# A hybrid attention and pooling layer on one core: key and query splits in other slots of GpSimd, VectorE and ScalarE, and a token load later in the first up step

## The reference, cut to what matters

```python
h = rmsnorm(x, norm1_g)
proj = h @ w_in                      # 8 query heads, 2 key and 2 value heads of 64, and 512 pooling columns
q = apply_axial_rope(rmsnorm(q, q_norm_g), cos, sin)
k = apply_axial_rope(rmsnorm(k, k_norm_g), cos, sin)
a = block_swept_gqa(q, k, v)         # softmax(q k^T / 8) v, bidirectional, 4 query heads share a key head
p = multiscale_pool(u, w_pool, pool_scale)
x = x + jnp.concatenate([a, p], axis=-1) @ w_out
h2 = rmsnorm(x, norm2_g)
x = x + jnp.square(jax.nn.relu(h2 @ w_up)) @ w_down
```

## Time and profile before

| what | before |
|---|---|
| median of 3 runs | 1506.07 us |
| lowest and highest | 1505.72 and 1506.11 us |
| the profiled execution's own time | 1507.0 us |
| its span, first to last instruction | 1505.2 us |
| TensorE busy | 1492.5 us, 99% of the span |
| VectorE, ScalarE, GpSimd busy | 68%, 48%, 26% |
| granted TensorE clock, mean | 1.000 |

### The profile page before, as it was taken

One profiled execution on the slowest core, in us unless ns is written; L12 is line 12 of the kernel. 1 busy time (PEld: TensorE's weight loads), 2 busy tenths in 40 slices (PEclk: granted clock), 3 DMA queues, 4 the chain that ended last, 5 costly groups with the idle time before them and its releaser, 6 DMA issues.

```text
span 1505.2 us, 23418 instructions
## 1 busy us (share of the span) xinstructions
PE 1492.5 (99%) x8035; PEld 1329.2 (88%) x8035; DVE 1018.7 (68%) x1287; ACT 717.6 (48%) x1212; POOL 391.7 (26%) x344
## 2 busy tenths in 40 slices
PE   9999999999999999999999999999999999999999
PEld 8999977888878889999999999999888888888887
DVE  7434489999975668445445444547888878888875
ACT  6323278999943445545455455546333223223220
POOL 3356368888950000000000000000411311311300
PEclk9999999999999999999999999999999999999999
DMA  6110021000054747533432433338743443443434
GB/s 241 46 34 18 18 84 36 12 14 10 15 189 168 256 154 290 233 127 115 151 138 111 152 120 122 130 137 309 277 154 107 145 153 98 142 158 93 149 99 181
DMA packets 68969, 195.19 MB, mean 130 GB/s; under 512 B 5544, under 2 KB 7728, under 8 KB 68784
## 3 DMA queue, kind: packets, MB, share of 16 engines
q1 hardware_dynamic: 66848, 183.36, 34.8%
q10 hardware_dynamic: 2064, 11.08, 1.8%
HBM read 119.97 MB, written 67.63 MB: 125 GB/s over the span
## 4 chain that ended last, share of the span: by engine, by line
PE 58%; DVE 0%; issue 0%; ACT 0%; DVEq 0%; ACTq 0%
PE ps L786 19%; PE ps L788 19%; PE ps L787 19%; DVE wulo L1706 0%; DVE hout L2091 0%; DVE wuraw L2033 0%; DVE yacc L2172 0%; ACT hout L1533 0%; ACT u L1221 0%; DVE u L2079 0%; DVEq L2076 0%; DVEq L2087 0%; DVEq L2236 0%; ACTq L1516 0%; DVEq L2077 0%
## 5 line engine op out<-in xcount | busy, mean ns | idle before, releaser
L786 PE MATMUL ps<-h,wuhi 128*128 128x384 f32 (+1 forms) x904 | 301.5, 334 | 1.0 <-ACT u L1221 0.8
L788 PE MATMUL ps<-h,wulo 128*128 128x384 f32 (+1 forms) x904 | 301.1, 333 | 0.0
L787 PE MATMUL ps<-h,wuhi 128*128 128x384 f32 (+1 forms) x904 | 301.1, 333 | 0.0
L786 PE MATMUL ps<-wdhi,hidhi 128*128 128x512 f32 x672 | 261.5, 389 | 0.0
L788 PE MATMUL ps<-wdhi,hidlo 128*128 128x512 f32 x672 | 261.5, 389 | 0.0
L787 PE MATMUL ps<-wdlo,hidhi 128*128 128x512 f32 x672 | 261.4, 389 | 0.0
L2165 DVE TENSOR_TENSOR yacc<-yacc,ps 128x1024 f32<-128x1024 f32 x167 | 203.3, 1217 | 77.6 <-PE ps L788 77.5
L1221 ACT ACTIVATE hidhi<-hin 128x1024 fp32r<-128x1024 f32 (+1 forms) x72 | 86.8, 1206 | 301.0 <-PE ps L788 292.0
L2079 DVE TENSOR_TENSOR u<-u,ps 128x384 f32<-128x384 f32 x96 | 53.1, 553 | 183.0 <-PE ps L788 178.5
L786 PEld LDWEIGHTS ps<-h,wuhi 128*128 128x128 f32 x904 | 169.7, 188 | 2.0 <-issue 1.4
L787 PEld LDWEIGHTS ps<-h,wuhi 128*128 128x128 f32 x904 | 169.7, 188 | 0.0
(11 more groups left out here) (217 smaller groups left out, 2821.2 us busy)
## 6 DMA issues: line engine op xcount, KB each, us to landing
hd<-hout SPq DMA_DIRECT2D x64, 384.0 KB, 3.2
hin<-hd SPq DMA_DIRECT2D x48, 512.0 KB, 3.7
hd<-hout SPq DMA_DIRECT2D x32, 576.0 KB, 2.8
hin<-hd SPq DMA_DIRECT2D x24, 768.0 KB, 4.3
wuraw<-in_w_up SPq DMA_DIRECT2D x17, 1024.0 KB, 5.9
wdraw<-in_w_down SPq DMA_DIRECT2D x8, 2048.0 KB, 9.5
h<-h2d ACTq DMA_DIRECT2D x7, 1536.0 KB, 10.2
xin<-in_x SPq DMA_DIRECT2D x12, 512.0 KB, 3.4
```

Of the source, the lines that this page charges most:

```text
L786: pe.matmul(out, w_hi, m_hi, start=start, stop=False, skip_group_check=resumed)
L787: pe.matmul(out, w_hi, m_lo, start=False, stop=False, skip_group_check=resumed)
L788: return pe.matmul(out, w_lo, m_hi, start=False, stop=stop, skip_group_check=resumed)
```

## The change

- SyncE: the two copies of the sample's key head 0 are issued one before each `move_out` of prompt pair 1. Both copies of key head 1 are issued behind the `move_out` of job 1 of the first sample pair.
- ScalarE: `split_q` of prompt pair 3 comes later, its first head behind the exponentials of slot 5 in pair 0, its second in slot 1 of pair 1. In the first up step `load_h2(4)` is issued behind the third `square_relu`, not before the first weights.
- VectorE: `split_q(2, 0)` goes to GpSimd, and `split_q(2, 1)` waits for it, so that `q_lo[0]` counts in order. `split_q(3, 0)` moves from slot 6 to the end of slot 7. `split_k(1, 1)` goes to GpSimd.
- GpSimd: takes `split_q(2, 0)` behind its first window step of the attention. `split_k(1, False)` moves from pair 0 to the end of prompt pair 3, and `split_k(1, True)` is added behind the window step of the first sample job.

```diff
@@ SyncE
             for pair in range(NQ // 2):
                 for half in range(2):
                     if pair == 1:
-                        double_k(1, half, False)
-                        if half == 0:
-                            double_k(1, 0, True)
+                        double_k(1, 0, half)
                     move_out(seqs[0], pair, 0, half)
-                if pair == 2:
-                    double_k(1, 1, True)
-            with sp.Fori(0, NQ // 2 - 1) as pair:
+            for idx in range(4):
+                move_out(seqs[1], 0, idx, idx % 2)
+                if idx == 1:
+                    for low in range(2):
+                        double_k(1, 1, low)
+            with sp.Fori(1, NQ // 2 - 1) as pair:
@@ ScalarE, attend
+                        if s.n == 0 and pair == 1 and k == 1:
+                            split_q(s, 3, 0, 1)
                         if exped_in(s, pair, idx, k) and not (last and (idx, k) == (2, 3)):
                             exps(*exped_in(s, pair, idx, k))
+                        if s.n == 0 and pair == 0 and k == 5:
+                            split_q(s, 3, 0, 0)
                         if s.n == 0 and pair == 0 and k == 4:
                             split_q(s, 2, 0, 1)
-                        if q_split_in(s, pair, idx, k):
+                        if q_split_in(s, pair, idx, k) and not (s.n == 0 and pair == 0):
@@ ScalarE, first_step
                 save_u(0, 0, 2)
-                load_h2(4)
                 hi_wu(1, 0)
                 hi_wu(1, 1)
                 square_relu(0, 0, 1)
                 hi_wu(1, 2)
                 square_relu(0, 0, 2)
+                load_h2(4)
@@ VectorE, split_q
                 dve.wait_ge(q_hi, 2 * pair + unit + 1)
+                if (pair, unit) == (2, 1):
+                    dve.wait_ge(q_lo[0], 5)
@@ VectorE, attend
-                        if s.n == 0 and pair == 3 and k == 0:
-                            dve.wait_ge(k_lo, NKV + 1)
-                            split_k(1, 1)
...
                         if s.n == 0 and pair < 2 and k == 4:
                             split_q(2 + pair, 1)
+                        if s.n == 0 and pair == 0 and k == 7:
+                            split_q(3, 0)
...
-                        if k == 6:
-                            q_split = q_split_in(s, pair, idx, 4)
-                            if q_split and q_split[0].n == 0:
-                                split_q(q_split[1], 0)
@@ VectorE, before attend
             split_p(seqs[0], 0, 0, 1)
-            split_q(2, 0)
@@ GpSimd
+            pool.wait_ge(win_step, done)
+            pool.wait_ge(q_hi, 5)
+            pool.wait_ge(q_lo[0], 4)
+            pool.tensor_tensor(Qs[64:, 0], QT[0:64, 2, 0:SEQ_P], Qs[0:64, 0].bitcast(F32), ALU.subtract).then_inc(q_lo[0], 1)
+            pool.wait_ge(q_lo[0], 5)
             normalize(seqs[0], 1, 0, 0)
...
                             split_k(0, False)
-                            split_k(1, False)
                             split_k(0, True)
...
+                        if s.n and (pair, idx) == (0, 0):
+                            pool.wait_ge(win_step, done)
+                            split_k(1, True)
...
+                        if s.n == 0 and pair == 3:
+                            split_k(1, False)
```

## The result

The changed kernel takes 1510.28 us (median of 7 runs, 1509.98 to 1513.72), the kernel before 1506.11 (median of 7 beside it, 1505.72 to 1507.23). The ratio is 1.0032, with a 95% interval of 1.0022 to 1.0042. That is slower by 4.2 us where 4.4 were forecast (1510.5, range 1507.2 to 1512.0). The profiled execution took 1510.28 us, its span is 1508.5 us, and its mean granted clock is 0.998.

The account below looks back on a forecast made before the run. TensorE was taken to bound the kernel, busy 1492.5 of 1505.2 us. Terms -3.2 (GpSimd) +1.4 (key split) +4.2 (copies' wait) +2.0 (clock) = +4.4 on 1506.07 gave 1510.5 us, range 1507.2 to 1512.0.

Parts of the forecast that it names:

- The step that decides: Opening of sample job 2: TensorE waits for key copies queued behind job 1's move_out; cost 4.2 us, 3.9 to 4.6.
- Rival 2: Sample job 2: the copies' wait is covered; 1504.3 us, or 1502.9 with GpSimd's 1.4 hidden too; chance 0.07.
- The clock: Behind the copies' wait: TensorE's clock falls and about 4.5 us run at half speed; cost 2.0 us, 0 to 3.5.
- rival 1: Copies' wait in the sample: the clock holds through the stall; +2.4 us, 1508.5 us; chance 0.33.
- Prompt, VectorE and ScalarE: Prompt pairs 0 to 2: moved query splits and key roundings remove TensorE stalls; gain 2.2 us by end of pair 1.
- Keys off VectorE: Prompt pair 3: split_k(1, 1) leaves VectorE, TensorE's 0.58 us at 247.52 goes; GpSimd's normalization beside it gets 1.05 back.
- GpSimd decides at the sample's first transposes: At 254.00: GpSimd's arrival, not TensorE's, sets the gain; 3.2 us, bounds 2.2 to 4.1.
- Rival 4: Prompt: GpSimd's part worth only 2.2 us, so the sum is +5.4, 1511.5 us; no chance given.
- Keys' low part on GpSimd in the sample: First sample job: split_k(1, True) ahead of normalizations takes 2.46 us against 1.05 slack; cost 1.4, 0.9 to 2.4.
- The token load: First up step: later load_h2(4) changes nothing; 0, bounds a gain of 0.9 us and a loss of 0.4.
- rival 3: First up step: the load does move behind the store; 0.9 us less, 1509.6 us; chance 0.15, alongside either other.

Follow-up runs that it names:

- experiment 1: Changed kernel with both copies of the sample's key head 1 issued behind the output move of sample job 0 instead of job 1: 1503.63 us.
- experiment 2: Changed kernel with TensorE's first sample pair unrolled and its wait for the key head 1 copies left out there: 1504.30 us.
- experiment 6: Kernel before with only the keys' part of the change (splits on GpSimd, copies moved), queries and token load as before: 1511.88 us.
- experiment 8: Kernel before with one DMA moved: the copy of key 1's low half behind the second sample job's output: 1511.04 us.
- experiment 4: Changed kernel, first sample pair unrolled, with 18 unused matmuls of 512 columns ahead of TensorE's wait for the copies: 1511.39 us.
- experiment 5: Changed kernel with the token load put back ahead of the first hi_wu: 1509.72 us.
- experiment 9: Kernel of experiment 1 with GpSimd's window step of the first sample job put one job later: 1505.52 us.
- experiment 10: Changed kernel, copies left in place, with GpSimd's window step of the first sample job put one job later: 1512.90 us.
- experiment 3: Kernel before with only the token load load_h2(4) moved behind the third squared sum: 1506.16 us.

## Why the prediction was right

- **The step that decides**, the place of the copies in SyncE's queue, held: experiments 1, 2, 6 and 8 each take it away or make it alone, and the time follows by 5 to 7 us. Rival 2 (the wait is covered) falls.
- **Its size**: 4.71 against 4.2, outside the bounds of 3.9 to 4.6. Of the working, the issue stood right: `o_full` starts 2.05 earlier (276.01), and the `KB` copy 1.78 after it, where 1.7 were reckoned. The landing was mis-sized, 3.6 for 3.1. The 3.1 was the median of two `KB` copies of before that were not alike: the one at 220.96, issued 0.8 us behind a `KA` copy, took 3.4, and the one at 246.71, alone, 2.8. The moved copy is of the first kind (alone it takes 3.0, experiment 8). With 3.4 the sum would have said 4.5.
- **The clock**: 2.05 to 2.16 against 2.0, and rival 1 (it holds) falls, by the window at 0.50, by the clock of all seven executions and by experiment 4. The reason given for the size is half right. In every profile the loss is about half of the time that TensorE works at the low level, as reckoned. But this time is 4.5 us only in the changed kernel and in experiment 5 (losses 2.16 and 2.14). In 6, 8 and 9 it is 3.4 us and costs 1.6 to 1.7, in 10 it is 2.9 and costs 1.4. Nor is the 2.6 us from the last matmul to the fall, by which rival 1 was weighed, a fixed figure: in the stalls of this study it is 2.2 to 5.2. In experiment 6 it was longer than the stall, and the clock fell all the same. So that the size was met owes something to luck.
- **Prompt, VectorE and ScalarE**: 0.58 for 0.57, 0.66 for 0.75 and 1.0 to 1.2 for 0.86: 2.45 together for 2.2. The mark at 216.80 kept 0.37 of its 0.39, so that the 0.4 of it was not won there; nearly all of the 0.66 came at 219.66, whose mark is gone. No run takes ScalarE's roundings apart from the other edits of the queries.
- **Keys off VectorE** 0.59 for 0.58, and the normalization beside it back at 1.12 us. The Trainium skill, "SBUF — State Buffer", section "Who interferes with whom", says that these two engines lock each other out of a shared port. Both cases agree with it: 2.89 to 0.94 us on VectorE, and 2.17 to 1.12 on GpSimd.
- **GpSimd decides at the sample's first transposes**: 3.54 (without the 0.15 from the start) for 3.2, and TensorE still waits there (0.71). The view was right and 0.3 small. Rival 4 (2.2 only) falls.
- **Keys' low part on GpSimd in the sample**: 1.67 for 1.4. The slack was 0.8, not 1.05. Experiments 9 and 10 show the cause.
- **The token load**: 0, as forecast, by experiments 3 and 5. The prediction took the stall of 602.90 for a property of the kernel. In four of the five profiles with the load in its old place it isn't there, and the median doesn't move with the load (experiment 3), so rival 3 (0.9 won if the load gets behind the store) has nothing to win. The profile after alone would have misled: the stall is gone there.
- **The sum**: -3.54 + 1.67 + 4.71 + 2.05 = +4.9 by 285.71. Later places take 0.3 back by 331.14 and 0.4 from 602.90 on, where the stall of before's profile takes another 0.9 of the offset. The median says +4.2. That 4.4 met it within 0.3 owes something to errors that cancel: the prompt's gain was too small by 0.34, and the losses by 0.3, 0.5 and up to 0.2.

## What to carry to other kernels

Follow a moved DMA in its queue to what stands ahead of it, and to every wait on its semaphore. Here one copy of 256 KB behind one `move_out` cost 5 us, more than all that the splits had won, because a wait written for later pairs holds in the first pair too. When work is taken out of a tight job, ask where the whole chain behind it lands: a window step moved by one job won 1.7 us and lost 3.1 and more 130 us later, until the chain was made to catch up. Before a stall in one profile is put into a sum, look whether other executions have it. And take a transfer's time from the row that had the same company: in the profiles of this study a `KB` copy issued 0.6 to 0.8 us behind a `KA` copy took 3.4 to 3.6 us, one alone 2.8 to 3.0.

## What of the hardware was not expected

- The clock can fall after TensorE has started again. In experiment 6 the engine was idle for 4.5 us, started at 283.47 with the clock at 1.00, and worked at 0.50 from about 284.2; in 8 and 9 too the fall came 0.4 and 0.5 us after the start. In the changed kernel, after the same wait as in 6, the clock had fallen by 279.2, while it still waited. Equal waits cost 2.16 and 1.64.
- Waits with marks of 2.94 us (experiment 9) and 3.33 us (8) brought such a fall too, waits of up to 1.57 us (the one for GpSimd at 273.89 and its like in experiment 5) did not. What a wait between these does, no run shows. At 2.94 it differs between executions: in the profile of experiment 10 the wait at the same place, with the same mark, has no fall behind it, and in 9 four executions of eleven show the fall in their mean clock.
- An up step early in the MLP has in some executions a stall of about 1 us for `u`, at one of two places (602.90 or 617.54 of before), with the same code. The stores that ScalarE waits for there share the transfer engines with 1536 KB loads.
